# Token slots of a pair's upper expert: numbered from 127 downwards instead of from 64 upwards

## The reference: one block of a hybrid network

```python
group_p = softmax(xf @ w_group_router);  g_w, g_idx = top_k(group_p, 1)      # 8 groups
e_w, e_idx = top_k(softmax(in_group), TOP_K)                                 # 2 of 8 in the group
gate = g_w * (e_w / sum(e_w));  expert = g_idx * 8 + e_idx
y_block = (silu(x_blk @ w_up[e][:, :256]) * (x_blk @ w_up[e][:, 256:])) @ w_down[e]
h = h + sum over a token's two experts of gate * y
```

```
26 41 27 34 11 21 20 26 30 35 24 43 36 21 40 31 20 14 23 29 17 20 24 15 44 38 35 34 38 38 54 37
```

```
38 37 24 42 28 30 33 24 38 41 52 45 40 35 48 53 21 17 19 11 9 16 19 18 37 35 52 54 43 36 38 69
```

## Time and profile before

| | us |
|---|---|
| median of three runs | 1331.26 |
| lowest, highest | 1330.52, 1333.41 |
| the profiled execution, device time | 1330.41 |
| its span, first to last instruction | 1328.5 |
| TensorE busy | 1132.4 (85%) |
| VectorE busy | 626.9 (47%) |
| ScalarE busy | 321.5 (24%) |
| GpSimd busy | 245.8 (19%) |

### The profile page before, as it was taken

One profiled execution on the slowest core, in us unless ns is written; L12 is line 12 of the kernel. 1 busy time (PEld: TensorE's weight loads), 2 busy tenths in 40 slices (PEclk: granted clock), 3 DMA queues, 4 the chain that ended last, 5 costly groups with the idle time before them and its releaser, 6 DMA issues. The chain is left out here.

```text
span 1328.5 us, 16794 instructions
## 1 busy us (share of the span) xinstructions
PE 1132.4 (85%) x6245; PEld 733.0 (55%) x6246; DVE 626.9 (47%) x928; ACT 321.5 (24%) x691; POOL 245.8 (19%) x347
## 2 busy tenths in 40 slices
PE   6999899998788876998978888888888888882996
PEld 5888788876767765887433333333333333322885
DVE  5699999984778765231811111111111111125674
ACT  5212211115555534221311000000010010022332
POOL 4000100003676640001112111111211111101120
PEclk9999999999899997999989999988999898895998
DMA  6111111100000106121999999999699999977431
GB/s 210 32 48 33 47 49 48 48 16 1 1 2 2 65 1 209 70 95 41 413 387 425 427 424 423 421 416 402 280 421 424 421 425 418 415 308 269 142 126 64
DMA packets 70243, 281.22 MB, mean 212 GB/s; under 512 B 12649, under 2 KB 38442, under 8 KB 53546
## 3 DMA queue, kind: packets, MB, share of 16 engines
q1 hardware_dynamic: 57120, 258.53, 49.1%
q0 software_dynamic: 9456, 16.80, 3.3%
q10 hardware_dynamic: 3610, 5.11, 1.1%
HBM read 268.34 MB, written 29.62 MB: 224 GB/s over the span
## 5 line engine op out<-in xcount | busy, mean ns | idle before, releaser
L2542 PE MATMUL ps_u<-wup,xgT 128*64 128x512 f32 x1024 | 262.8, 672 | 57.6 <-DMA wup<-in_w_up_dram 55.2
L2542 PEld LDWEIGHTS ps_u<-wup,xgT 128*64 128x64 f32 x1024 | 87.6, 153 | 231.2 <-issue 230.0
L2411 DVE TENSOR_TENSOR hb<-sil,ps_u 128x256 f32<-128x256 f32 x32 | 13.5, 421 | 310.3 <-ACT sil L2316 310.3
L94 PE MATMUL ps_b<-n_hi,wh 128*128 128x512 f32 x384 | 157.6, 411 | 0.7 <-DVE wl L431 0.7
L94 PE MATMUL ps_b<-n_hi,wl 128*128 128x512 f32 x384 | 151.9, 396 | 0.0
L94 PE MATMUL ps_b<-n_lo,wh 128*128 128x512 f32 x384 | 151.7, 395 | 0.0
L94 PE MATMUL ps_y<-wg_hi,hx 128*128 128x512 f32 x256 | 82.5, 399 | 2.5 <-DVE hx L2484 2.5
L2316 ACT ACTIVATE sil<-ps_u 128x256 f32<-128x256 f32 x32 | 12.3, 384 | 297.6 <-PE ps_u L2542 297.6
L94 PEld LDWEIGHTS ps_b<-n_hi,wh 128*128 128x128 f32 x384 | 73.3, 191 | 16.5 <-issue 2.6
L94 PEld LDWEIGHTS ps_b<-n_hi,wl 128*128 128x128 f32 x384 | 72.8, 190 | 16.3
L94 PEld LDWEIGHTS ps_b<-n_lo,wh 128*128 128x128 f32 x384 | 73.3, 191 | 15.0 <-issue 1.0
(11 more groups left out here) (373 smaller groups left out, 1879.6 us busy)
## 6 DMA issues: line engine op xcount, KB each, us to landing
wup<-in_w_up_dram SPq DMA_DIRECT2D x64, 2048.0 KB, 17.4
zT<-in_w_down_dram SPq DMA_DIRECT2D x32, 1024.0 KB, 18.1
convT<-in_w_down_dram SPq DMA_DIRECT2D x32, 1024.0 KB, 17.4
wraw<-in_w_in_dram SPq DMA_DIRECT2D x24, 512.0 KB, 4.2
convT<-y_rows SPq DMA_DIRECT2D x16, 512.0 KB, 4.7
qkvT<-in_x_dram SPq DMA_DIRECT2D x8, 512.0 KB, 8.5
qkvT<-in_w_out_dram SPq DMA_DIRECT2D x8, 512.0 KB, 5.3
xr<-in_x_dram SPq DMA_DIRECT2D x8, 512.0 KB, 3.8
```

The lines of the kernel that those rows point to most:

```text
L94: ins = nc.tensor.matmul(ps, lhs[a], rhs[b], start=first and k == 0, stop=last and k == 2)
L2411: nc.vector.tensor_tensor(hb[k][rows], sil[k][rows], ps_u[k][rows, FE:2 * FE], ALU.mult).then_inc(s_h, 1)
L2542: last = nc.tensor.matmul(ps_u[k][HC[c], :], xgT[k][:, j, HC[c]], wup[k][c][:, j, :], start=j == 0, stop=j == NJ - 1)
```

## The change

Before, iP holds 0 to 127. Now its first 64 entries are 0 to 63 and the others 127, 126, ..., 64. Slot numbers are computed as before; the position where iP equals the slot is another one. Token number i of an upper expert (i from 0) has slot 64 + i; it was at position 64 + i and is now at 127 - i. Positions of lower experts and of overflow blocks are unchanged. An upper expert with 38 tokens filled positions 64 to 101 and left 102 to 127 empty; now it fills 127 down to 90 and leaves 64 to 89 empty. Since iP takes two iota instructions, the waits on `s_iota` count one more.

```diff
@@ -1871,7 +1871,7 @@
-                dve.wait_ge(s_iota, 9)
+                dve.wait_ge(s_iota, 10)
@@ -1956,16 +1956,17 @@
                 def iota(t, pattern, base, mult):
-                    nc.gpsimd.iota(t[:], pattern, base=base, channel_multiplier=mult, allow_small_or_imprecise_dtypes=True).then_inc(s_iota, 1)
-                iota(i8, [[1, 8]], 0, 0)
-                iota(i64, [[1, NE]], 0, 0)
-                iota(iP, [[1, P]], 0, 0)
-                iota(iN, [[1, NIP]], 0, 0)
-                iota(val, [[P, NT], [T, 2]], 1, 1)
+                    nc.gpsimd.iota(t, pattern, base=base, channel_multiplier=mult, allow_small_or_imprecise_dtypes=True).then_inc(s_iota, 1)
+                iota(i8[:], [[1, 8]], 0, 0)
+                iota(i64[:], [[1, NE]], 0, 0)
+                iota(iP[:, 0:C], [[1, C]], 0, 0)
+                iota(iP[:, C:P], [[-1, C]], P - 1, 0)
+                iota(iN[:], [[1, NIP]], 0, 0)
+                iota(val[:], [[P, NT], [T, 2]], 1, 1)
...
-                pool.wait_ge(s_iota, 8)
+                pool.wait_ge(s_iota, 9)
@@ -2038,7 +2039,7 @@
-                pe.wait_ge(s_iota, 9)
+                pe.wait_ge(s_iota, 10)
```

## The result

The changed kernel took 1334.98 us, the median of 20 runs (1333.04 to 1340.16), the kernel before in its own 20 runs 1333.03 us. The ratio is 1.0019 with a 95% interval of 1.0010 to 1.0028. Taken as independent the two make 1.0018, give or take 0.0007: a loss of 2.4 us, give or take 0.9. It lies within the 0.2% that the forecast called no change, and inside the range, but it is not nothing: both intervals exclude 1. The measured 1334.98 is 3.6 us above the forecast of 1331.4; 1.8 of these are that the kernel before itself has a median of 1333.03 over 20 runs, where the three runs shown had 1331.26.

What follows compares the result with a forecast made beforehand. The expert stage was taken to run at the pace of DMA transfers, each complete with its slowest engine. Profiled 1330.4 + 0.1 + 0 = 1330.5 us, in terms of the shown runs' median (0.85 higher) 1331.4; range 1327 to 1336.5.

Steps and rivals of the forecast that it cites:

- The iota: Start of routing: two iotas of 64 columns for one of 128 delay the select by 0.11 us; 0.1 us taken.
- Unequal engines as the pace of the stage: Expert stage: a transfer completes when its slowest engine does; uneven token rows are worth over a microsecond per pair.
- the tail of rows 7: After the last weights' issue: busy share falls stepwise from 1178, the last two or three engines busy some 12 us longer.
- The cap: Most that evenly spread rows could gain: 6.5 us for each of two tails, 13 us.
- Rows 8: Ahead of the last tail: issuing two ordinary 0.5 MB loads kept SyncE 10.70 us, read as full queues at late engines.
- Deal A: Gathers and scatters: each half has eight engines of its own, four positions at a time; mirrored, largest load stays 166 rows.
- deal B: Gathers and scatters: engine is position modulo 16 over both halves; change 8.6 us faster, part of the faster rival, chance 0.13.
- C: Gathers and scatters: four positions at a time over 16 engines both halves share; part of the faster rival, chance 0.13.
- The mirror gives exactly 0: Gathers and scatters: numbering from the top mirrors the upper eight engines' loads, largest stays 166 rows, 0 us; chance 0.69.
- slower, late engine: Expert stage: upper half's heaviest load moves to a possibly slower engine; 5 us in the middle, at most 10; chance 0.14.
- rows 5: Steady stretches of the stage: busy share 1.01 at 424 and 414 GB/s, 2.4%, giving the slow side's bound, some 10 us.
- the later entry to the stage: First two gathers share engines with the p projection's last stores; up to 8 more rows, 1.3 us; chance 0.04.

Runs made afterwards that it cites:

- e4: Changed kernel with other upper iota: tokens keep the engines of the kernel before, empty rows come first on each engine; 1332.37 us, 1.0002 of before.
- e8: Changed kernel with other iotas: tokens dealt in turn to each half's eight engines, every other group of eight backwards; 1321.22 us, 0.9899 of before.
- e1: Changed kernel with one iota instead: consecutive tokens of an expert go in turn to the eight engines of their half; 1318.58 us, 0.9888 of before.
- e10: Changed kernel with both halves concentrated in groups of eight tokens, lower from its first engine, upper from its last; 1355.27 us, 1.0184 of before.
- e5: Changed kernel with upper groups of eight tokens starting at the last but one upper engine, then downwards, last gets leftovers; 1354.86 us, 1.0174 of before.
- e2: Changed kernel with upper half concentrated: groups of eight tokens fill engines from the first upper one, lower half as before; 1353.74 us, 1.0152 of before.
- e6: Changed kernel with lower half concentrated from its first engine in groups of eight tokens, upper half as before the change; 1350.84 us, 1.0133 of before.
- e3: Changed kernel with upper half concentrated: groups of eight tokens fill engines from the last upper one, lower half as before; 1357.32 us, 1.0181 of before.

## Why the prediction was right or wrong

**The iota** was sized right up to VectorE: 0.07 us in the trace for 0.11 forecast. That it reaches the sum is not shown. At the entry of the stage 0.3 us came with it in the profile, within what a single execution tells, but e4 has two iotas too and enters at 39.69 us against 39.70 before, and in e8 0.8 us of iota left 0.07.

**Unequal engines as the pace of the stage**, read from the tail of rows 7, was right and is now shown from both sides: 101 rows fewer on the heaviest engine, 15 us faster; 106 more, 20 us slower; the same largest load in either half or in both, ratios from 1.0133 to 1.0184. The cap, the idle share of the two tails, 6.5 us each and 13 in all, is not refuted: e1 brought 15, by its interval 12 to 17. Rows 8, read as full queues in front of late engines, were no evidence of unequal loads, since SyncE was held 12.94 us in e1.

**Deal A**, chosen by the form of the tail, held. Under deal B the change itself would have spread the rows and been 8.6 us faster, under C faster still; it was not. And e1 was laid out by deal A and gained what A said. The same count of rows under the other deals fails: under B the largest load of e1 would be 198 + 160 against 173 + 137 before, and e1 would be slower; under C that of e10 would fall from 272 + 224 to 166 + 132, and e10 would be faster. The section "The descriptor swizzle" of the Trainium skill's page "DMA: Bandwidth & Descriptors" gives deal A for a plain transfer. The runs agree with it for these indirect ones as to which positions share an engine; the number of an engine no run here shows.

**The mirror gives exactly 0** is the term that was mis-sized, by 2.4 us. It rests on "with equal engines", and where a load stands did matter: concentrated, it costs 3.9 us more at the upper half's last engine than at its first. The rival "slower, late engine" named the direction and, it may be, the cause; its price was put at 5 us in the middle and 10 at most, and the loss is 2.4. I gave it 0.14 and the exact mirror 0.69. The forecast of no change stands as to size, since 2.4 us is just under 0.2%, but the better sum was the mirror plus a small loss. Nothing in the rows of the kernel before gave its value: the 424 and 414 GB/s of rows 5 are two stretches of one kernel, 2.4% apart, and over the whole stretch behind the overflow block the two kernels differ by 0.7%. Against the rival I argued that the tail fits with 16 equal engines. That was no argument, since the engine in question was then among the lightest. Whether that engine is slow in itself is not shown: what both pairs of traces have in common is the later entry to the stage, the place that the prediction gave 0.04 and 1.3 us.

The Trainium skill, same page, section "Latency and other measured facts", calls engines 7 and 15 "usually slower". For the last upper engine, 15 by its deal, the runs agree in sign, with 0.29% when it carries 512 rows; e5 leaves open whether it is that engine alone, and the rival of unlike places whether it is the engine at all. For the last lower one, 7, no run here shows it clear of noise.

**What the change was worth** lay elsewhere. Numbering downwards permutes loads among engines and lowers none. The same table with another order, e1, lowers the largest and beats both kernels: 1318.58 us, 1.1% faster than before.

What stays open: why a load on the last upper engine costs more, whether by the engine, by the entry to the stage or by unlike places of the heaviest; whether e5's engine shares it; and whether a row costs more on an overloaded engine (by the medians 0.19 us in e2 and 0.16 in e6, against 0.15 in e1).

## What to carry to other kernels

When the DMA engines bound a stage, look at how the busy share falls off once the queue is empty: here a long thin tail meant that a few engines carried more, and the load of the heaviest set the pace of the stage. Rows that are often empty should then be placed so that the full ones go round the engines; a mirror image of the same heap only changes which engine carries it, which here cost 0.2% and gained nothing. In comparing two profiles, first measure a stretch in which both programs are the same: here it held 2.7 of 4.5 us.

## What the runs showed of the hardware

An empty slot of an indirect transfer costs little but is there: with the completion marks 5360 of the 9456 packets of that queue. If a real row takes the 0.157 us that 4 KB of weights take, they share what is left of the queue's 705 engine-us, an estimated 0.01 us each. One engine with more work does not hold up the others at once: in the kernel before the share stayed at 1.01 although the loads behind the overflow block differed by 108 rows, 16 us; only with a largest load of 272 + 224 did it fall, to 0.97 to 0.99 (e2, e3). TensorE's granted clock behind the overflow block was 0.94 in e1, where weights came fastest, and 0.91 in e2 and e3, where they came slowest; between those it did not follow the rate (0.92 at 422 GB/s before, 0.93 at 419 in the changed kernel).
